# A trunk step with routed experts: the residual as rows in DRAM, expert outputs weighted and scattered with addition, experts, overflow and final norm in one block

## What is computed

```python
h = x + mix                                    # mix = merged @ w_out
xf = rms_norm(h, norm_ffn_g)
...
def block_fn(args):
    xb, e = args
    h = jax.nn.silu((xb @ w_gate[e]).astype(f32)) * (xb @ w_up[e]).astype(f32)
    return h.astype(dt) @ w_down[e]
...
out = jnp.zeros((T, x.shape[1]), f32).at[row_tok].add(ybuf.astype(f32) * row_w[:, None])
...
y = rms_norm(h + ffn, norm_final_g)
```

## Time and profile before

| | |
|---|---|
| median of 3 runs (lowest, highest) | 1986.24 us (1983.44, 1988.4) |
| the profiled execution | 1989.84 us, span 1988.0 us |
| mean granted clock of TensorE | 0.953 |
| TensorE busy | 1787.1 us, 90% of the span |
| VectorE, ScalarE, GpSimd busy | 1068.0, 776.6, 522.3 us |
| DMA | 315.77 MB, mean 159 GB/s |

### The profile page before, as it was taken

How to read it: one execution, slowest core, us unless ns; L and a number is a source line. 1 busy time by engine, 2 the same in 40 slices (tenths; PEclk the granted TensorE clock), 3 DMA queues, 4 the chain that set the end, 5 groups by cost and what they waited for, 6 DMA issues and landing times. The chain is left out here.

```text
span 1988.0 us, 26737 instructions
## 1 busy us (share of the span) xinstructions
PE 1787.1 (90%) x10064; PEld 1554.8 (78%) x10064; DVE 1068.0 (54%) x1220; ACT 776.6 (39%) x940; POOL 522.3 (26%) x317
## 2 busy tenths in 40 slices
PE   5999979999999999999799979939999999999950
PEld 4898869999999999999699968726777777677730
DVE  6565560001455444545511133247888989888837
ACT  5545550001122111122200032227777777777732
POOL 1322222232222222232123200022443333233310
PEclk8999989999999999999899989959999999999985
DMA  3111102223111111110123373138999999999927
GB/s 126 51 45 47 47 21 64 64 67 117 45 46 32 34 45 34 34 44 22 35 86 97 115 259 127 48 123 304 375 385 384 380 383 381 365 384 385 389 94 266
DMA packets 144859, 315.77 MB, mean 159 GB/s; under 512 B 10508, under 2 KB 105948, under 8 KB 119036
## 3 DMA queue, kind: packets, MB, share of 16 engines
q1 hardware_dynamic: 134940, 283.95, 40.1%
q0 software_dynamic: 9856, 30.98, 4.5%
HBM read 291.79 MB, written 30.97 MB: 162 GB/s over the span
## 5 line engine op out<-in xcount | busy, mean ns | idle before, releaser
L229 PE MATMUL job_ps<-xn_hi,w_hi 128*128 128x352 f32 x1536 | 508.0, 331 | 8.6 <-issue 2.6
L231 PE MATMUL job_ps<-xn_hi,w_lo 128*128 128x352 f32 x1536 | 495.5, 323 | 0.0
L230 PE MATMUL job_ps<-xn_lo,w_hi 128*128 128x352 f32 x1536 | 494.8, 322 | 0.0
L1761 DVE TENSOR_TENSOR ex_w_lo<-u,ex_w_hi 128x2048 fp32r<-128x2048 f32 x128 | 290.1, 2287 | 35.7 <-ACT ex_w_hi L1709 35.5
L213 POOL CAST w_hi<-w_raw 128x1024 fp32r<-128x1024 f32 x80 | 87.0, 1087 | 829.1 <-PE job_ps L231 391.6
L229 PEld LDWEIGHTS job_ps<-xn_hi,w_hi 128*128 128x128 f32 x1536 | 289.9, 189 | 13.1 <-issue 8.4
L230 PEld LDWEIGHTS job_ps<-xn_lo,w_hi 128*128 128x128 f32 x1536 | 290.9, 189 | 0.9
L231 PEld LDWEIGHTS job_ps<-xn_hi,w_lo 128*128 128x128 f32 x1536 | 289.8, 189 | 0.0
L1709 ACT ACTIVATE ex_w_hi<-u 128x2048 fp32r<-128x2048 f32 x128 | 245.3, 1918 | 73.1 <-PE ex_gate L1639 34.5
L215 POOL TENSOR_TENSOR w_lo<-w_raw,w_hi 128x1024 fp32r<-128x1024 f32 x80 | 215.6, 2695 | 6.4
L1761 DVE TENSOR_TENSOR ex_w_lo<-ex_raw,ex_w_hi 128x2048 fp32r<-128x2048 f32 x64 | 145.8, 2280 | 1.5 <-ACT ex_w_hi L1709 1.5
(11 more groups left out here) (267 smaller groups left out, 2942.3 us busy)
## 6 DMA issues: line engine op xcount, KB each, us to landing
u<-in_w_chunks SPq DMA_DIRECT2D x128, 1024.0 KB, 9.1
ex_raw<-in_w_chunks SPq DMA_DIRECT2D x64, 1024.0 KB, 8.2
w_raw<-in_w_in SPq DMA_DIRECT2D x64, 512.0 KB, 4.4
co_y<-y_rows POOLq DMA_DIRECT2D x8, 1024.0 KB, 8.2
merged_lru<-ml_merged SPq DMA_DIRECT2D x8, 528.0 KB, 3.1
mr_old<-merged_lru SPq DMA_DIRECT2D x8, 528.0 KB, 4.3
merged<-mr_merged SPq DMA_DIRECT2D x8, 528.0 KB, 3.1
x_tile<-in_x_prompt SPq DMA_DIRECT2D x8, 512.0 KB, 4.7
```

The costliest lines, as they stand in the source:

```text
L229: pe.matmul(out, self.w_hi[s][:, k, :], x_hi[:, k, cols], start=(k == 0), stop=False)
L230: pe.matmul(out, self.w_hi[s][:, k, :], x_lo[:, k, cols], start=False, stop=False)
L231: mm = pe.matmul(out, self.w_lo[s][:, k, :], x_hi[:, k, cols], start=False, stop=(k == KD - 1))
L1761: dve.tensor_tensor(w_lo[n % SPLIT][:], H.raw[n % RAW], w_hi[n % SPLIT][:].bitcast(F32), ALU.subtract).then_inc(lo_done, 1)
```

## The change

- `out_proj` is written out tile by tile. The `x` tile becomes the residual in place, in a ring of three (`XR`), and GpSimd stores it as `h_rows` in DRAM ahead of `xf_rows`. `H.h` is gone; its SBUF becomes four more raw buffers, `H.more`, of which the ring of chunks now uses all eight (`RAW`). SP loads chunks 4 to 7 at once behind the first tiles and chunks 0 to 3 after the split as before.
- The router makes one list (row to gather, 32 columns instead of 64), and a second set of products gives each slot its weight (`H.w_slot`). `weigh_gates` moves ahead of the slots, `weigh_slots` behind `x_part(0)`; the weight products stand in step 0.
- ScalarE multiplies with the slot's weight as it copies an expert's output. GpSimd scatters these rows into `h_rows` with addition, one expert after the other: an add waits for the one before (`y_added`). The gather and the add share one list of rows in a ring of four (`ROWS`), so the gather of expert e also waits for the add of e - 4.
- The last expert: its chunks are split ahead of `out(30)`, and `down_last` does the left half and then the right half, each into a bank of its own, so that the left is copied while the right is multiplied.
- `overflow` and `combine` become parts of the experts' block. The final norm reads `h_rows` (1056 rows) in nine loads into nine buffers, ScalarE squares, VectorE scales in place, SP stores. The state rows are stored early.

```diff
+        XR = 3
...
+                load_m(0)
+                load_m(1)
+                for t in range(XR):
+                    load_x(t)
+                for c in range(4, Chunks.RAW):
+                    load_chunk(sp, A, H, *Chunks.ORDER[c], c)
...
+                for t in range(2, NTILE):
+                    load_m(t)
+                    if t >= XR:
+                        load_x(t)
...
+                    pool.wait_ge(h_done[1], t + 1)
+                    pool.dma_start(h_rows[span(t), :], hx[t % XR][0:n, :]).then_inc(h_stored[t % XR], 16)
...
+                dve.wait_ge(rt_in, 80)
+                split(1)
...
+            weigh_gates(dve, st)
...
+        def weigh_slots(dve):
+            for k in range(2):
+                dve.tensor_tensor(hw[k][:], hot[k][:], wide(w[k], E), ALU.mult).then_inc(hw_done, 1)
...
-            st.link(dve.tensor_copy(H.over[:], over_f[:]))
+            dve.tensor_copy(H.over[:], over_f[:]).then_inc(self.over_set, 1)
...
+        def scalar_weights(act):
+            act.wait_ge(w_turned, 1)
+            act.activation(H.w_slot[:], pw, ACT.Copy).then_inc(self.weights_out, 1)
+            act.wait_ge(self.weights_out, 1)
+
+        def tensor_weights(pe):
+
+            for k in range(2):
+                pe.wait_ge(hw_done, k + 1)
+                for t in range(NTILE):
+                    n = P if t < NT else DEC
+                    mm = pe.matmul(pw, in_slot[k][0:n, t, :].bitcast(F32), hw[k][0:n, t, :],
+                                   start=(k == 0 and t == 0), stop=(k == 1 and t == NT))
+            mm.then_inc(w_turned, 1)
...
-    RAW = 6
+    RAW = 8
...
+                sp.wait_ge(y_added, 16 * E)
+                sp.wait_ge(ov_passed, 1)
+                for t in range(NTILE):
+                    sp.dma_start(fin[t][0:n_rows(t), :], h_rows[span(t), :]).then_inc(h_in[t], 16)
+                for t in range(NTILE):
+                    sp.wait_ge(out_done, t + 1)
+                    dst = y_prompt[0, span(t), :] if t < NT else y_sample[0]
+                    sp.dma_start(dst, fin[t][0:n_rows(t), :]).then_inc(out_stored, 16)
...
+                    if e >= ROWS:
+                        pool.wait_ge(y_added, 16 * (e - ROWS + 1))
+                    pool.tensor_copy(row[e % ROWS][:], H.slots[:, e:e + 1]).then_inc(row_set, 1)
+                    pool.wait_ge(row_set, e + 1)
...
+                    if e:
+                        pool.wait_ge(y_added, 16 * e)
                     pool.indirect_dma_start(
-                        out=y_rows, out_offset=bass.IndirectOffsetOnAxis(ap=row_out[b][:], axis=0), in_=y[b][:],
-                        in_offset=None, bounds_check=2 * T - 1, oob_is_err=False).then_inc(y_stored[b], 16)
-
-                for b in range(2):
+                        out=h_rows, out_offset=bass.IndirectOffsetOnAxis(ap=row[e % ROWS][:], axis=0),
+                        in_=y[e % 2][0:SLOTS, :], in_offset=None, bounds_check=T - 1, oob_is_err=False,
...
+                def down_last(e):
+
+                    pe.wait_ge(h_lo_done, e + 1)
+                    for m, out in enumerate((pg, pu)):
+                        at = slice(m * 512, m * 512 + 512)
+                        for i, c in enumerate((4, 5)):
+                            n = AT[e, c]
+                            pe.wait_ge(lo_done, n + 1)
+                            hi = w_hi[n % SPLIT][:].rearrange("p (k n) -> p k n", k=2)
+                            lo = w_lo[n % SPLIT][:].rearrange("p (k n) -> p k n", k=2)
+                            for k in range(2):
+                                kk = 2 * i + k
+                                ins = three(out[0:SLOTS, :], h_hi[:, kk, :], h_lo[:, kk, :], hi[:, k, at], lo[:, k, at],
                                             kk == 0, kk == KF - 1)
...
+                    if s == 0:
+                        router.tensor_weights(pe)
+                    elif s < E:
                         down(s - 1)
+                    else:
+                        down_last(LAST)
...
+                def out_half(e, m, src):
+                    act.activation(y[e % 2][0:SLOTS, m * 512:m * 512 + 512], src[0:SLOTS, :], ACT.Copy,
+                                   scale=H.w_slot[:, e:e + 1]).then_inc(y_done, 1)
 
                 def out(e):
-                    b = e % 2
-                    act.wait_ge(used, chunks.at[e, 5] + 1)
+                    act.wait_ge(used, AT[e, 5] + 1)
+                    if e == 0:
+                        router.scalar_weights(act)
                     if e >= 2:
-                        act.wait_ge(y_stored[b], 16 * (e // 2))
+                        act.wait_ge(y_added, 16 * (e - 1))
                     for m in range(N2):
-                        act.activation(y[b][:, m * 512:m * 512 + 512], py[m][:], ACT.Copy).then_inc(y_done, 1)
+                        out_half(e, m, py[m])
...
+                hi(LAST, 4)
+                hi(LAST, 5)
+                h_part(LAST)
+                out(LAST - 1)
+                act.wait_ge(y_added, 16 * (LAST - 1))
+                for m, src in enumerate((pg, pu)):
+                    act.wait_ge(used, AT[LAST, 4 + m] + 1)
+                    out_half(LAST, m, src)
...
+                act.activation(warm[:], R.eps[0:1, :], ACT.Sqrt)
+                for t in range(NTILE):
+                    n = n_rows(t)
+                    act.wait_ge(h_in[t], 16)
+                    act.activation(junk[0:n, :], fin[t][0:n, :], ACT.Square,
+                                   accum_out=ss[0:n, t:t + 1]).then_inc(sq_done, 1)
+                    act.wait_ge(sq_done, t + 1)
+                    act.activation(rms[0:n, t:t + 1], ss[0:n, t:t + 1], ACT.Sqrt, bias=R.eps[0:n, :],
+                                   scale=1.0 / D).then_inc(rms_done, 1)
...
+                lo(LAST, 4)
+                lo(LAST, 5)
+                h_part(LAST)
...
+                    dve.scalar_tensor_tensor(out=fin[t][0:n, :], in0=fin[t][0:n, :], scalar=rstd[0:n, t:t + 1],
                                              in1=g_fin[0:n, :], op0=ALU.mult, op1=ALU.mult).then_inc(out_done, 1)
```

More of the change, by code:

```diff
@@ L1142, in out_proj @@
         h_done = [sem(f"h_done{n}") for n in range(2)]
+        h_stored = [sem(f"h_stored{b}") for b in range(XR)]
         sq_done, rms_done = sem("sq_done"), sem("rms_done")
@@ L1152, in out_proj @@
         N2 = D // 512
[L1154 to L1158, removed]
-                for b in range(2):
[L1160 to L1180, removed]
+        rows = lambda t: P if t < NT else DEC
+        span = lambda t: slice(t * P, t * P + rows(t))
         with nc.Block() as block:
@@ L1260, in logits @@
                     mm.then_inc(logit_done, 1)
[L1262 to L1272, removed]
-                with pe.Fori(1, NT // 2) as i:
-                    both(i * 2, 0, P)
-                    both(i * 2 + 1, 1, P)
@@ L1276, in _ @@
-                both(NT, 0, DEC)
-                turn(NT, 0, DEC)
-                logits(NT, DEC)
+                for t in range(NTILE + 1):
+                    if t < NTILE:
+                        project(t, 0)
+                    if t == 1:
+                        pe.wait_ge(rt_in, 80)
+                    if t:
+                        turn(t - 1)
+                    if t < NTILE:
+                        project(t, 1)
+                    if t:
+                        logits(t - 1)
@@ L1313, in _, with split @@
                 act.wait_ge(init, 1)
-                two_ahead(act, split, norm, weights)
+                weights(range(0, 3))
+                split(0)
+                weights(range(3, KD))
+                split(1)
+                for t in range(NTILE):
+                    norm(t)
             @block.vector
             def _(dve):
-                def split(t, b, i, n):
+                def split(t):
+                    b, n = t % 2, rows(t)
                     dve.wait_ge(m_hi_done, t + 1)
@@ new lines, in experts @@
+        ov_gu_done, ov_silu_done, ov_hid_done = osem("gu_done"), osem("silu_done"), osem("hid_done")
+        ov_h_turned, ov_h_out, ov_y_done = osem("h_turned"), osem("h_out"), osem("y_done")
+        ov_w_copied, ov_weighed, ov_added, ov_put = osem("w_copied"), osem("weighed"), osem("added"), osem("put")
+        ov_passed = osem("passed")
+        fsem = lambda n: ctx.enter_context(nc.semaphore(f"fi_{n}"))
+        fin = [R.u[:, t * D:(t + 1) * D] for t in range(NT)] + [H.more[:, 0:D]]
+        warm = sb("fi_warm", [1, 1])
@@ new lines, in over_experts, with listed, over_tiles @@
+        def over_experts(eng, each):
+            eng.wait_ge(router.over_set, 1)
+            n_over = eng.value_load(H.over[0:1, E:E + 1], min_val=0, max_val=E)
+            with eng.If(n_over > 0):
+                with eng.Fori(0, n_over) as i:
+                    each(i)
+            eng.nop()
+        def listed(eng, i):
+            return eng.value_load(H.over[0:1, ds(i, 1)], min_val=0, max_val=E - 1)
+        def over_tiles(eng, i, body):
```

(14 more changed lines are left out.)

644 lines of the change are left out of this document (268 added, 376 removed).

## The result

The changed kernel took 1976.62 us (median of 5, 1975.0 to 1976.98) against 1987.42 us before on the same chip (median of 5, 1983.44 to 1988.4): a ratio of 0.9947, 95% interval 0.9933 to 0.9962. That is faster beyond the interval, but only by 0.5%: 10.8 us, where 29.5 were forecast. The spans of the two profiled executions, 1988.0 and 1974.9 us, differ by 13.1 us.

The account below looks back on a forecast made before the run. TensorE was taken to set the experts' pace with DMA almost full, then a 65.7 us tail; -7.0 - 36.0 + 11.2 + 3 - 0.7 = -29.5 us from 1986.2 gave about 1957 us, range 1942 to 1981.

Parts of the forecast that it names:

- Out-projection: Output projection: four more early chunks beside GpSimd's router weights and g_ffn cost 3 us, between 0 and 8.
- My own condition: Output projection: the forecast is wrong if early chunks hold up the router's weights by more than 8 us.
- Router: Router: narrower slot matmuls gain 0.7 us; the added weight products cost zero, falling into TensorE's wait for rows.
- Adds: Experts: adding rows to DRAM needs 8.65 MB more reads, 25.6 us of DMA time, 11.2 us after three covers.
- The price of 0.80 us an expert: Experts: DMA time for the adds' reads, from the row traffic's share of the queue, 2.96 us per MB.
- my dear bound: Experts: adds priced by the backlog's growth, 5.6 us per MB, cost 34 us after covers; 1980 us, 18% chance.
- the share of the queue: Experts: basis chosen to price the adds, gather and plain scatter taking 8.5% of 556 us for 15.97 MB.
- Two buffers as cover: Experts: two more raw buffers filled ahead hide 5.5 us of the adds' DMA time, 2.74 us per chunk.
- GpSimd's chain: Experts: gather of s+2 waits for the add of s-2; costs nothing. Slower rival: long landings, 2008 us, 10% chance.
- Last expert: Last expert: splitting both chunks first leaves 1.7 us idle and gains 7.0 us, or 4.2 if the clock falls.
- Tail: From last matmul to end: shrinks from 65.7 to 29.7 us, a gain of 36.0 us.
- the DMA's path: Tail: 8.65 MB read and written at 380 GB/s takes 22.8 us, ending at 29.7 us, after the engines' 28.3.

Follow-up runs that it names:

- Kernels 1 and 2: Changed kernel with chunks 4 to 7 issued late, 1963.4 us; with all eight chunks early but merged tile 2 loaded behind the first four, 1967.08 us.
- the twelfth run: Changed kernel with chunks 4 to 7 late and VectorE's first three splits waiting until GpSimd copied two experts' row numbers and issued the first gather; 1958.17 us.
- kernels 3 and 4: Scatter as a plain write without addition, in the changed kernel, 1959.57 us, and in that with chunks 4 to 7 issued late, 1944.75 us.
- kernel 7: Changed kernel with chunks 4 to 7 late and eight row-number buffers instead of four, so gathers wait for older adds; 1963.73 us.
- Kernel 9: Changed kernel with chunks 4 to 7 late and a plain scatter, plus one extra gather of the same rows beside each scatter; 1998.15 us.

## Why the forecast was too large, step by step

**The step that failed is "Out-projection".** It took 3 us, between 0 and 8, and looked for what the four early chunks would hold up among GpSimd's loads, the router's weights and `g_ffn`. Those were hardly late. What was late is the load that stands on the chunks' own queue: merged tile 2, behind eight chunks. The four chunks of before had already left it only 4.7 us late for ScalarE, hidden by TensorE's work on tile 1; four more put 11.3 us on top, ScalarE's queue carried them to the turned rows of tile 0, and TensorE lost 9.7 us in idle time and 3.3 more in busy time, at the slower clock. Kernels 1 and 2 take this back, each with all eight buffers filled ahead. My own condition ("hold up the router's weights by more than 8 us") named the wrong load.

**Router.** -0.7 forecast, +1.8 found. From the issue of the first gather to the first turning are 8.1 us instead of 6.6: 1.5 of it. The twelfth run shows that this gather lands in 4.1 us when it is issued ahead of the refilling chunks, but no run shows why it is slower behind them than in the kernel before.

**Adds.** The forecast was +11.2 us against before, and +9.8 came; but two errors lie in that agreement. The price of 0.80 us an expert was too low: in the twelve experts in which the DMA bound (1622.68 to 1737.59 and 1812.43 to 1924.07 us) the mean period is 18.88 us, 1.21 above 17.67, which makes 14.5 us; the growth of landings gives 1.0. The price by the backlog's growth, my dear bound, was 5.6 us per MB or 1.5 an expert: the truth lies about halfway between, and I should have kept both rows in the sum, not the share of the queue alone. Against it, 15 experts passed before anything waited, and the period with the stall of the overflow list became 2.3 us shorter (21.8 instead of 24.1), which nothing in the forecast held. Two buffers as cover: 5.5 forecast, 6.5 and 7.3 measured. The Trainium skill's halved rate for an add (Collectives: The Full Stack, The bandwidth ceiling) would double the scatter's 0.80 us, as my sum did; 1.0 to 1.2 measured on top of it says a little worse than half, if the scatter itself costs 0.80, which no run here shows. Its 425 GB/s for a large load (DMA: Bandwidth & Descriptors, Bandwidth) would have made the adds free; kernels 3 and 4 show that they are not, and the stage moved 380 to 388 GB/s before and 366 to 372 after.

**GpSimd's chain.** Costed at nothing, and kernel 7 confirms it. But the room was smaller than said. I had drawn the loop over two experts with 13.5 to 14.4 us for an add; on GpSimd's own queue it spans one: scatter, landing, copy, gather, scatter. The changed kernel's waits show the true slack, (109.4 - 18.5) / 27 = 3.4 us per expert on average, so by estimate an add landing some 3 us later would already have set the pace. Kernel 9 shows it: a landing 1.5 us later and one more issue with its wait, 2.9 us, are 4.4 in all.

**Last expert.** -7.0 forecast, -3.9 found: the idle time of 1.76 us was right, but its chunks were late (some 1.2 us) and the clock fell for a moment (1.9 us). With the plain scatter the stretch is 30.8 us, 6.6 less than before, and the last down takes 5.8 us after the same 1.76 us of idle time: the step was right where the DMA is not behind. Why the clock fell in the one and not in the other stays open.

**Tail.** 31.7 us against 29.7. The add landed in 5.2 us instead of 4.5, the first tile in 3.6 instead of 4.9, and from the last VectorE op to the end it takes 6.5 us where the DMA's path left 3.9: 0.7 - 1.3 + 2.6 make the 2 us. The mechanism was right: the engines are done at 1968.4, and what is left is the DMA's, whose share is 1.0 from 1955 to 1972 us.

Sum of the misses: 10.1 in the projection, 2.5 in the router, -1.4 in the experts, 3.1 in the last one, 2.0 in the tail and 0.2 ahead of them are, but for rounding, the 16.4 us between -29.5 and -13.1.

## What to carry to other kernels

When transfers are issued earlier, list first what comes behind them on the same queue, with the time that each already waits, and only then what shares the DMA from other queues: here one load with four chunks fewer ahead of it was worth 13 us of the stretch. Where a stretch runs at a DMA share of 1.0, price added traffic by how fast the backlog grows and not by the queue's share of busy time, and count covers (buffers filled ahead) separately, for both errors can cancel. A loop through one engine's queue must be drawn in the order of its instructions, not by data alone.

## What the runs showed of the hardware

- 66 rows of 4 KB added to DRAM landed in 9.9 us under load (median) where a plain scatter of them took 8.2 to 8.3, and cost a saturated DMA 1.0 to 1.2 us; gathering the same rows cost 2.1 us or more. The queue's share, 12.4% with adds and 8.8% without over 1400 to 1800 us, puts only 0.65 us on each. Where the rest goes is open.
- A GpSimd copy of 96 numbers took 6.49 us beside three VectorE splits of 2.3 us each, and 0.18 us without them.
